# The MLP's down projection as seven quarter products, with the sums of weight quarters on POOL

## The chip, the cores and the metric

The kernel runs on one core of a Trainium2 chip. A run's time is device microseconds (us) from launch to end. The kernel before took 1097.14 us, the median of three runs (1096.91 to 1100.08). "Same" below means within 0.3% of it.

## What is computed

Two layers over 528 tokens (16 meta tokens and 512 of the sequence), width 1024, everything in float32. Each layer has an attention and pooling mixer, and then a gated MLP whose inner width is 2816 (22 blocks of 128). Cut to the part that is changed:

```python
xn = rms_norm(h, ffn_norm_g[l])
g = causal_dwconv(xn @ w_gate[l], conv_w[l], conv_b[l])          # width 3
h = h + (jax.nn.gelu(g, approximate=False) * (xn @ w_up[l])) @ w_down[l]
# after layer 1: return h[:, N_META:]
```

## The kernel before

The five engines run their own programs and meet through semaphores: PE multiplies, ACT and DVE do elementwise work, POOL does some more of it, SP only issues the loads. The order on each engine is the order in which the code is written; there is no scheduler.

**Every large product is three.** PE multiplies in fp32r, so each operand is kept as a rounded part and the rest: `w_hi` and `w_lo` for weights, `x_hi`/`x_lo` and `m_hi`/`m_lo` for activations. `dense` issues, for each block of 128 rows and 128 output features, hi·hi, hi·lo and lo·hi, each for both halves of the tokens (264 columns in a matmul), or in layer 1 in one matmul of 512 columns where only real tokens matter.

**Weight units.** Weights come in units of 256 output columns and up to 8 row blocks. SP loads unit u into `raw[u % 2]`; `split_hi` (ACT) writes `w_hi`, `split_lo` (DVE) subtracts and writes `w_lo`. A slot is rewritten when PE has finished the unit two before.

**The MLP.** Eleven turns i, each with four output tiles on PE: gate0, gate1, up0, up1 (PSUM slots 2, 3, 0, 1). DVE moves the gate tiles out of PSUM, ACT and DVE make the convolution in `conv`, ACT applies GELU, DVE moves the up tiles out, POOL multiplies (L774), and ACT and DVE split the product into `m_hi` and `m_lo`, which hold all 22 blocks. PE is meanwhile at the next turn.

**Down.** After the eleven turns, `w_down` is used in 12 units: four column pairs j, each with 8, 8 and 6 row blocks. The first units need only blocks 0 to 15 of `m`, so the chain behind the last up tile is under them. A finished tile is added to the residual `h` by DVE (`add_to_h`); in layer 0 ACT and DVE then at once make the next layer's operands `x_hi`, `x_lo` and the sum of squares (`gain_hi`, `gain_lo`, `square`, `add_square`), a column pair at a time.

Of the kernel before, what the change touches and what calls it, by code (L numbers as in the profile page):

```python
# [31 lines left out]
P = 128  # L32
# [18 lines left out]
U_DOWN = U_FFN + 2 * FI  # L51
DOWN_K = [(0, 8), (8, 16), (16, FT)]
UNITS = U_DOWN + len(DOWN_K) * (D_MODEL // UC)

# [11 lines left out]
class Psum:  # L66
# [7 lines left out]
    def __init__(self):  # L74
# [9 lines left out]
        order += [(f"down{t}", (2 + t) % 4) for t in range(KT)]  # L84
# [18 lines left out]
def build_trunk(nc, x, meta_tokens, attn_norm_g, w_in, q_norm_g, k_norm_g, sinks, w_pool, pool_scale,  # L103
# [5 lines left out]
    with ExitStack() as ctx:  # L109
# [64 lines left out]
        with ExitStack() as sc:  # L174
            m_hi = sb(sc, "m_hi", [P, FT, L], f32r)
            m_lo = sb(sc, "m_lo", [P, FT, L], f32r)
            gate = [sb(sc, f"gate{c}", [P, 2 + L]) for c in range(2)]
            conv = [sb(sc, f"conv{c}", [P, L]) for c in range(2)]
            up = [sb(sc, f"up{c}", [P, L]) for c in range(2)]
            cpar = sb(sc, "cpar", [P, 4, 2])  # L180
# [27 lines left out]
        down_used = sem("down_used")  # L208
# [32 lines left out]
        dve_par, dve_rot, dve_attn, dve_ffn = sem("dve_par"), sem("dve_rot"), sem("dve_attn"), sem("dve_ffn")  # L241
# [57 lines left out]
        def slot_turn(l, unit, pairs=0):  # L299

            return l * (UNITS // 2) + pairs + unit // 2

        def unit_rows(unit):
            if unit == U_POOL:
                return 2
            if unit >= U_DOWN:
                a, b = DOWN_K[(unit - U_DOWN) % 3]
                return b - a
            return 8

        def last_user_done(l, unit, i=0):


            old = unit - 2
            if old < 0:
                if old + UNITS == UNITS - 1:
                    name = f"down{KT - 1}"
                    return filled[ps.slot(name)], ps.before_last_layer(name, l) + 1
                return down_used, l * KT + 1
            if old >= U_DOWN:  # L320
                j, n = divmod(old - U_DOWN, 3)
                if n < 2:
# [8 lines left out]
            return filled[ps.slot(name)], ps.before(name, l, i) + 1  # L331


        def split_hi(act, l, unit, i=0, half=None):
# [11 lines left out]
        def split_lo(dve, l, unit, i=0, half=None):  # L346
# [3 lines left out]
            s, t, nk = unit % 2, slot_turn(l, unit, i), unit_rows(unit)  # L350
# [20 lines left out]
        def _(sp):  # L371
# [9 lines left out]
            def load(l, unit, src, i=0):  # L381

                s, n = unit % 2, unit_rows(unit)
                parts = [(raw[s][:, a:a + n // 2], src[:, a:a + n // 2]) for a in (n // 2, 0)]
                sp.wait_ge(lo_split[s], slot_turn(l, unit, i) + 1)
                for dst, part in parts:
                    sp.dma_start(dst, part).then_inc(raw_loaded[s], 16)

            for l in range(DEPTH):
# [10 lines left out]
                sp.wait_ge(lo_split[s], slot_turn(l, U_POOL) + 1)  # L400
# [5 lines left out]
                for j in range(D_MODEL // UC):  # L406
                    load(l, U_OUT + j, wo[:, :, j * UC:(j + 1) * UC])
                with sp.Fori(0, FI) as i:
                    load(l, U_FFN, wg[:, :, bass.ds(i * UC, UC)], i)
                    load(l, U_FFN + 1, wu[:, :, bass.ds(i * UC, UC)], i)  # L410
                for j in range(D_MODEL // UC):
                    for n, (a, b) in enumerate(DOWN_K):
                        load(l, U_DOWN + 3 * j + n, wd[:, a:b, j * UC:(j + 1) * UC])

# [10 lines left out]
        def _(pe):  # L425
# [40 lines left out]
            pe.sem_inc(down_used, 1)  # L466
# [25 lines left out]
            for l in range(DEPTH):  # L492
# [156 lines left out]
                with pe.Fori(0, 2) as i:  # L649
                    for t in range(4):  # L650
                        s, unit = open_slot(f"out{t}", l, i), U_OUT + t // 2
                        if t % 2 == 0:
                            pe.wait_ge(lo_split[unit % 2], slot_turn(l, unit, i) + 2)
                        dense(s, unit % 2, (t % 2) * P, rows, mix_hi, mix_lo, ready=mixed if t == 0 else None,
                              tail=l + 1 == DEPTH)\
                          .then_inc(filled[s], 1)


                def mlp_tiles(i, ready=None):
                    for n, name in enumerate(("gate0", "gate1", "up0", "up1")):  # L660
                        s, unit = open_slot(name, l, i), U_FFN + n // 2
                        if n % 2 == 0:
                            pe.wait_ge(lo_split[unit % 2], slot_turn(l, unit, i) + 2)
                        dense(s, unit % 2, (n % 2) * P, eight, x_hi, x_lo, ready=ready if n == 0 else None,
                              real=n >= 2 and l + 1 == DEPTH,
                              tail=n < 2 and l + 1 == DEPTH).then_inc(filled[s], 1)
                        if n == 0 and ready is not None:
# [711 lines left out]
```

## Time and profile before

| | |
|---|---|
| median of the runs | 1097.14 us |
| the profiled execution | 1099.67 us; its span, first to last instruction, is 1097.9 us |
| PE, DVE, ACT, POOL busy | 1061.1, 522.6, 471.5, 121.3 us |
| granted PE clock, mean | 0.987 of full speed |

A matmul is counted busy from its start to its modelled end, and matmuls overlap, so what one costs in a stream is the distance between two starts, not its duration. Each row of a timeline has the start (us from the span's start) and the duration; "x2" merges two instructions. In rows of a window the columns are named in the answer's second line: the stretch, its length, busy time and count, the granted clock, and the DMA share and rate.

### The profile page before, as it was taken

Reading aid. Unit: us, or ns where it says so; the run is one execution under the profiler, and the core shown is the slowest. Engines: PE = TensorE matmul, PEld = TensorE weight load, DVE = VectorE, ACT = ScalarE, POOL = GpSimd, SP = SyncE. Lnnn points to the kernel's source line nnn. Section 1 sums busy time; section 2 is a strip of 40 time slices with the busy share of each in tenths; the row PEclk is TensorE's granted clock in tenths of the full one; section 3 lists DMA queues with packets and bytes.
Section 4 is the critical chain, followed back from the end, with each engine's and each line's share of the span. In section 5 each row is a group of like instructions: output and inputs, shape, how many; then the busy total and the mean of one; then the engine's idle time right before and its main releaser. Section 6 shows DMA issues by size and latency. Waiting matters only on the chain.

```text
span 1097.9 us, 18457 instructions
## 1 busy us (share of the span) xinstructions
PE 1061.1 (97%) x7668; PEld 996.7 (91%) x7668; DVE 522.6 (48%) x690; ACT 471.5 (43%) x662; POOL 121.3 (11%) x121
## 2 busy tenths in 40 slices
PE   6898899999999999999999988999999999999997
PEld 6897799999999999999999878999988999888886
DVE  5566744545544545233336576455445454532221
ACT  5765536445434444122228655364354443421110
POOL 1252000011000011000002610000001100000000
PEclk8989999999999999999999999999999999999999
DMA  6311122232322232323231112322323232233212
GB/s 199 105 49 39 67 88 77 80 113 76 97 95 76 78 113 67 106 78 105 77 105 39 49 40 78 115 77 90 101 76 106 85 107 84 76 106 106 76 58 77
DMA packets 93518, 94.30 MB, mean 86 GB/s; under 512 B 3392, under 2 KB 91800, under 8 KB 93480
## 3 DMA queue, kind: packets, MB, share of 16 engines
q1 hardware_dynamic: 92768, 93.01, 26.6%
q0 software_dynamic: 400, 0.58, 0.2%
q8 instruction: 27, 0.44, 0.2%
q10 hardware_dynamic: 312, 0.18, 0.1%
q14 instruction: 11, 0.09, 0.0%
HBM read 91.65 MB, written 2.10 MB: 85 GB/s over the span
## 4 chain that ended last, share of the span: by engine, by line
PE 84%; ACT 7%; DVE 6%; DMA 1%; issue 1%; ACTq 0%; DVEq 0%
PE slot L451 82%; ACT probs L929 3%; DVE nmax L1180 1%; PE slot L507 1%; ACT w_hi L342 1%; DMA par_in<-in_conv_w 1%; DMA cst<-const_table 1%; DVE ms_work L1131 1%; DVE probs L1199 1%; DVE mix_lo L1215 0%; ACT x_hi L788 0%; DVE den L1191 0%; DVE sink_arg L1185 0%; ACT pool_hi L862 0%; ACT rot_s L854 0%
## 5 line engine op out<-in xcount | busy, mean ns | idle before, releaser
L451 PE MATMUL slot<-x_hi,w_hi 128*128 128x264 f32 (+2 forms) x1552 | 363.1, 301 | 6.8 <-DVE u_sb L1162 4.1
L451 PE MATMUL slot<-x_lo,w_hi 128*128 128x264 f32 (+2 forms) x1552 | 360.1, 299 | 0.0
L451 PE MATMUL slot<-x_hi,w_lo 128*128 128x264 f32 (+2 forms) x1552 | 359.3, 299 | 0.0
L353 DVE TENSOR_TENSOR w_lo<-raw,w_hi 128x2048 fp32r<-128x2048 f32 (+2 forms) x87 | 195.4, 2246 | 248.4 <-ACT w_hi L342 248.4
L342 ACT ACTIVATE w_hi<-raw 128x2048 fp32r<-128x2048 f32 (+3 forms) x89 | 160.8, 1807 | 263.1 <-PE slot L451 260.0
L451 PEld LDWEIGHTS slot<-x_hi,w_hi 128*128 128x128 f32 x1552 | 254.3, 191 | 19.2 <-DVE u_sb L1162 5.8
L451 PEld LDWEIGHTS slot<-x_lo,w_hi 128*128 128x128 f32 x1552 | 252.8, 191 | 7.3
L451 PEld LDWEIGHTS slot<-x_hi,w_lo 128*128 128x128 f32 x1552 | 252.4, 191 | 7.5
L451 PE MATMUL slot<-m_hi,w_lo 128*128 128x264 f32 (+1 forms) x528 | 140.7, 321 | 0.0
L451 PE MATMUL slot<-m_hi,w_hi 128*128 128x264 f32 (+1 forms) x528 | 140.4, 320 | 0.0
L451 PE MATMUL slot<-m_lo,w_hi 128*128 128x264 f32 (+1 forms) x528 | 140.3, 320 | 0.0
L774 POOL TENSOR_TENSOR up<-up,conv 128x528 f32<-128x528 f32 (+1 forms) x44 | 57.6, 1309 | 573.6 <-ACT conv L999 538.5
L994 ACT ACTIVATE conv<-gate,cpar 128x528 f32<-128x528 f32 (+1 forms) x44 | 36.2, 823 | 149.5 <-DVE gate L1088 75.6
L451 PEld LDWEIGHTS slot<-m_lo,w_hi 128*128 128x128 f32 x528 | 87.6, 188 | 7.9
L451 PEld LDWEIGHTS slot<-m_hi,w_lo 128*128 128x128 f32 x528 | 87.4, 188 | 7.6
L451 PEld LDWEIGHTS slot<-m_hi,w_hi 128*128 128x128 f32 x528 | 87.6, 188 | 7.4
L999 ACT ACTIVATE conv<-conv 128x528 f32<-128x528 f32 (+1 forms) x44 | 28.1, 639 | 73.7 <-DVE conv L1297 73.7
L451 PE MATMUL slot<-mix_hi,w_hi 128*128 128x264 f32 (+1 forms) x256 | 52.0, 284 | 0.0
L451 PE MATMUL slot<-mix_hi,w_lo 128*128 128x264 f32 (+1 forms) x256 | 51.9, 284 | 0.0
L451 PE MATMUL slot<-mix_lo,w_hi 128*128 128x264 f32 (+1 forms) x256 | 51.7, 284 | 0.0
L1088 DVE TENSOR_TENSOR gate<-slot,rinv 128x528 f32<-128x528 f32 x22 | 15.6, 708 | 56.6 <-PE slot L451 56.5
L1287 DVE TENSOR_TENSOR gate<-slot,rinv 128x516 f32<-128x516 f32 x22 | 15.3, 696 | 55.3 <-PE slot L451 55.2
(144 smaller groups left out, 941.7 us busy)
## 6 DMA issues: line engine op xcount, KB each, us to landing
raw<-in_w_gate SPq DMA_DIRECT2D x44, 512.0 KB, 4.6
raw<-in_w_up SPq DMA_DIRECT2D x44, 512.0 KB, 4.5
raw<-in_w_down SPq DMA_DIRECT2D x32, 512.0 KB, 4.4
raw<-in_w_in SPq DMA_DIRECT2D x19, 512.0 KB, 5.0
raw<-in_w_out SPq DMA_DIRECT2D x16, 512.0 KB, 4.1
raw<-in_w_down SPq DMA_DIRECT2D x16, 384.0 KB, 3.6
x_in<-in_x SPq DMA_DIRECT2D x4, 512.0 KB, 7.0
out<-y_out SPq DMA_DIRECT2D x8, 256.0 KB, 3.0
```

Of the source, the lines that this page charges most:

```text
L342: ins = nc.scalar.activation(w_hi[s][:, a:b], raw[s][:, a:b], ACT.Copy)
L353: ins = nc.vector.tensor_tensor(w_lo[s][:, a:b], raw[s][:, a:b], w_hi[s][:, a:b].bitcast(f32), ALU.subtract)
L451: ins = nc.tensor.matmul(out_part, w[ws][:, r, cols], a[:, k, tokens], start=first and n == 0 and w is w_hi and a is a_hi, stop=end and w ...
L507: ins = nc.tensor.matmul(slot[s][:, 0, 2 * b:2 * b + 2], head_sq[:, b, :], cst[:, C_BLK:C_BLK + P:HEAD_DIM], start=True, stop=True)
L774: nc.gpsimd.tensor_tensor(up[c][:, t0:], up[c][:, t0:], conv[c][:, t0:], ALU.mult)\
L929: ins = nc.scalar.activation(probs[:, y, t, 0:nk], slot[s][:, t // 2, col], ACT.Exp, bias=nm[:, y, t:t + 1], scale=q_scale[:, b, t // 2, t ...
L994: nc.scalar.activation(conv[c][:, t0:], gate[c][:, 2 + t0:], ACT.Identity, bias=cpar[:, 3, c:c + 1], scale=cpar[:, 2, c:c + 1]).then_inc(t ...
L999: nc.scalar.activation(conv[c][:, t0:], conv[c][:, t0:], ACT.Gelu).then_inc(gelu_ready, 1)
L1088: nc.vector.tensor_tensor(tok(dst), halves(s), tok(rinv[:]), ALU.mult).then_inc(evac[s], 1)
L1131: rot.link(nc.vector.reciprocal(ms_work[:], ms_work[:]))
L1180: ch.link(nc.vector.tensor_reduce(nmax[:, y].rearrange("p (a t) -> p a t", a=2), view, op=ALU.max, axis=AX.X, negate=True))
L1287: nc.vector.tensor_tensor(tok(gate[c][:, 2 + TAIL0:]), tail_halves(s), tok(rinv[:, TAIL0:]), ALU.mult).then_inc(evac[s], 1)
```

## The change

Down is done in three chunks of the inner width instead of at the end: after turns 0 to 3, 4 to 7 and 8 to 10 (`CHUNKS`), and in each chunk for four column pairs (`down` units, which the text calls d0 to d3). A unit of n turns is a 2 by 2 product of quarters: two blocks of output features, two halves of the tokens, and the two row blocks of each turn. It is computed with seven products of quarters (`PRODUCTS`, P1 to P7) where `dense` made eight; four of the seven weight operands and four of the seven activation operands are sums of quarters.

- POOL makes the weight sums (`operand_sums`: four instructions a unit, into one buffer `w_sum`), ACT and DVE split the seven weight operands in four groups (`operand_hi`, `operand_lo`, n = 0 to 3).
- DVE makes the activation sums of every turn (`middle_sums`, four instructions), ACT and DVE split into `m_op` in three parts.
- In the last turn of each chunk DVE, not POOL, does the gated product (`gated`).
- P1 and P6 and P7 share one PSUM bank and accumulate in it, P5 and P3 another. DVE adds each product to `h` (`add_product`), and the next product into that bank waits for this.
- All loops are written out; the tap of `conv` is a scaled Copy (before: Identity with bias), and the bias goes into GELU. `m_sum` lies in the buffer of `conv`.
- In layer 1 a quarter is 256 tokens wide, in layer 0 264.

```diff
-DOWN_K = [(0, 8), (8, 16), (16, FT)]
+CHUNKS = [(0, 4), (4, 8), (8, FI)]
+for c, (a, b) in enumerate(CHUNKS):
+    PLAN += [(kind, i) for i in range(a, b) for kind in ("gate", "up")] + [("down", 4 * c + j) for j in range(4)]
++PRODUCTS = {"P1": (0, 0, (0, 0), ((0, 0),)), "P2": (0, 1, (0, 1), ((0, 0),)), "P3": (2, 2, (1, 0), ((0, 1),)),
+            "P4": (3, 6, (1, 1), ((1, 0),)), "P5": (1, 3, (1, 0), ((1, 1),)), "P6": (1, 4, (0, 0), ((0, 1),)),
+            "P7": (2, 5, (0, 0), ((1, 0), (1, 1)))}
+ORDER = ("P1", "P5", "P2", "P6", "P3", "P4", "P7")
+FIRST_ORDER = ("P1", "P2", "P5", "P4", "P6", "P3", "P7")
```

In `PRODUCTS` each entry has the group of weight operands, the activation operand, the PSUM bank and the quarters of `h` it is added to. On PE:

```diff
+                def product(name, unit, kks, first, last):
...
+                    pe.wait_ge(opnd_lo[op], d + 1)
+                    if first and name in ("P6", "P3", "P7"):
+                        pe.wait_ge(h_added, added_count(d, {"P6": "P1", "P3": "P5", "P7": "P6"}[name]))
+                    for kk in kks:
+                        for n, (w, a) in enumerate(((0, 0), (0, 1), (1, 0))):
+                            ins = nc.tensor.matmul(dst, part[s][w][:, wn, kk], m_op[a][:, m, kk, 0:width],
+                                                   start=first and kk == kks[0] and n == 0 and name in ("P1", "P2", "P4", "P5"),
+                                                   stop=last and kk == kks[-1] and n == 2, skip_group_check=True)
...
+                        for name in FIRST_ORDER[0:4]:
+                            product(name, unit, range(n - 1), True, False)
+                        for name, parts in (("P1", 1), ("P2", 2), ("P5", 3), ("P4", 3)):
+                            pe.wait_ge(mlo_ready, 3 * (l * FI + i1 - 1) + parts)
+                            product(name, unit, range(n - 1, n), False, True)
+                        for name in FIRST_ORDER[4:]:
+                            product(name, unit, range(n), True, True)
```

On POOL, for every down unit (`operand_sums`):

```diff
+                    if part == 0:
+                        pool.wait_ge(raw_loaded[s], load_turn(l, unit) * 32 + 32)
+                        if d > 0:
+                            pool.wait_ge(opnd_lo[1], d)
+                        nc.gpsimd.tensor_tensor(sums[:, 0], a21, a22, ALU.add).then_inc(sum_ready, 1)
+                        pool.wait_ge(sum_ready, 4 * d + 1)
+                        nc.gpsimd.tensor_tensor(sums[:, 1], sums[:, 0], a11, ALU.subtract).then_inc(sum_ready, 1)
+                        return
+                    if d > 0:
+                        pool.wait_ge(opnd_lo[2], d)
+                    pool.wait_ge(sum_ready, 4 * d + 2)
+                    nc.gpsimd.tensor_tensor(sums[:, 2], a12, sums[:, 1], ALU.subtract).then_inc(sum_ready, 1)
+                    nc.gpsimd.tensor_tensor(sums[:, 3], a21, a11, ALU.subtract).then_inc(sum_ready, 1)
```

Three places in the engines' orders follow. First, **DVE in layer 0, from the second tap to the end of a turn of the loop.** Before (every turn; `up0` and `up1` are the up tiles, L353 is `split_lo`):

```order
L1294 SCALAR_TENSOR_TENSOR conv1<-gate1,cpar,conv1 128x528 [waits tap2_ready]
L1297 SCALAR_TENSOR_TENSOR conv1<-gate1,cpar,conv1 128x528 [waits dve_ffn]
L1088 TENSOR_TENSOR up0<-slot0,rinv 128x528 [waits filled0]
L1088 TENSOR_TENSOR up1<-slot1,rinv 128x528 [waits filled1]
L353 TENSOR_TENSOR w_lo1<-raw1,w_hi1 128x2048 [waits hi_split1]
L1312 TENSOR_TENSOR m_lo<-up0,m_hi 128x528
L1312 TENSOR_TENSOR m_lo<-up1,m_hi 128x528
```

After, in the last turn of chunk 0 (L445 is `operand_lo`, L1515 `gated`, `work` holds `up` and `conv`; `w_ext` and `w_lo` hold the operands):

```order
L445 TENSOR_TENSOR w_lo0<-w_sum,w_hi0 128x1024 [waits opnd_hi1]
L1293 TENSOR_TENSOR work<-slot0,rinv 128x528 [waits filled0,mlo_ready]
L1515 TENSOR_TENSOR work<-work 128x528 [waits evac0,gelu_ready]
L445 TENSOR_TENSOR w_lo0<-w_sum,w_hi0 128x1024 [waits opnd_hi2]
L445 TENSOR_TENSOR w_ext_lo0<-raw0,w_ext_hi0 128x512 [waits opnd_hi3]
L445 TENSOR_TENSOR w_ext_lo1<-raw1,w_ext_hi1 128x1024 [waits opnd_hi0]
L445 TENSOR_TENSOR w_ext_lo1<-raw1,w_ext_hi1 128x512 [waits opnd_hi3]
L1293 TENSOR_TENSOR work<-slot1,rinv 128x528 [waits filled1,mlo_ready]
L1515 TENSOR_TENSOR work<-work 128x528 [waits evac1,gelu_ready]
L1525 TENSOR_TENSOR work<-work 128x264 [waits m_last]
```

Four `operand_lo` now stand between the first and the second up tile, and the activation sums (from L1525) and three splits follow before PE may finish d0.

Second, **POOL in that last turn.** Before, a turn's two L774 (`up<-up,conv`) are all its work. After:

```order
L928 TENSOR_TENSOR work<-work 128x528 [waits evac1,gelu_ready]
L908 TENSOR_TENSOR w_sum<-raw0 128x512 [waits raw_loaded0]
L910 TENSOR_TENSOR w_sum<-w_sum,raw0 128x512 [waits sum_ready]
L915 TENSOR_TENSOR w_sum<-raw0,w_sum 128x512 [waits sum_ready]
L916 TENSOR_TENSOR w_sum<-raw0 128x512
L908 TENSOR_TENSOR w_sum<-raw1 128x512 [waits opnd_lo1,raw_loaded1]
L910 TENSOR_TENSOR w_sum<-w_sum,raw1 128x512 [waits sum_ready]
L915 TENSOR_TENSOR w_sum<-raw1,w_sum 128x512 [waits sum_ready,opnd_lo2]
L916 TENSOR_TENSOR w_sum<-raw1 128x512
```

The sums of d1 (raw1) start once DVE has made d0's group 1, and their second pair once it has made group 2: among the four `operand_lo` shown above.

Third, **DVE in the last chunk of layer 0, from d2 to d3.** Before, at the same stage (L1262 adds a finished tile to `h`, L1043 is `gain_lo`, L1053 `add_square`):

```order
L1262 TENSOR_TENSOR h<-slot2,h 128x528 [waits filled2]
L1262 TENSOR_TENSOR h<-slot3,h 128x528 [waits filled3]
L1043 SCALAR_TENSOR_TENSOR x_lo<-h,par_all,x_hi 128x528 [waits xhi_ready] x2
L1053 TENSOR_TENSOR sumsq<-sq 128x528 [waits sq_ready]
L353 TENSOR_TENSOR w_lo0<-raw0,w_hi0 128x2048 [waits hi_split0]
```

After (L1553 adds a product to `h`, L1248 is `gain_lo`, L1261 `add_square`; slots 2 and 3 belong to d2, 0 and 1 to d3):

```order
L445 TENSOR_TENSOR w_ext_lo1<-raw1,w_ext_hi1 128x384 [waits opnd_hi3]
L1553 TENSOR_TENSOR h<-slot3,h 128x264 [waits h_added,prod_done]
L1553 TENSOR_TENSOR h<-slot2,h 128x264 [waits h_added,prod_done]
L1553 TENSOR_TENSOR h<-slot2,h 128x264
L1248 SCALAR_TENSOR_TENSOR x_lo<-h,par_all,x_hi 128x528 [waits xhi_ready]
L1261 TENSOR_TENSOR sumsq<-sumsq,sq 128x528 [waits sq_added,sq_ready]
L1248 SCALAR_TENSOR_TENSOR x_lo<-h,par_all,x_hi 128x528 [waits xhi_ready]
L1261 TENSOR_TENSOR sumsq<-sumsq,sq 128x528 [waits sq_added,sq_ready]
L1553 TENSOR_TENSOR h<-slot0,h 128x264 [waits h_added,prod_done]
```

The next layer's splits stand between the last addition of d2 and the addition of d3's P1, for which PE's P6 of d3 waits.

## Rows read from the trace of the kernel before

**Rows 1.** The page's part 1, busy time of three engines.
```profile
PE 1061.1 (97%) x7668; PEld 996.7 (91%) x7668; DVE 522.6 (48%) x690; ACT 471.5 (43%) x662; POOL 121.3 (11%) x121
```
**Rows 2.** The chain that ended last, its two longest pieces: start, us, what.
```profile
182.72 392.46 PE slot L451 x3216
...
721.94 365.62 PE slot L451 x2064
```
**Rows 3.** Windows of PE: down in both layers, two gate tiles.
```profile
435.10:563.20 128.10, 128.10 (x1058) 1.00 0.28 92
965.50:1087.40 121.90, 121.90 (x529) 1.00 0.22 71
...
761.29:772.88 11.59, 11.59 (x97) 1.00 0.28 90
```
**Rows 4.** Groups by form: what one costs on ACT, DVE and POOL (mean ns).
```profile
L342 ACT ACTIVATE w_hi<-raw 128x2048 fp32r<-128x2048 f32 x75 | 143.3, 1911 | 195.3 <-PE slot L451 192.2 <-DMA cst<-const_table 3.0
...
L1043 DVE SCALAR_TENSOR_TENSOR x_lo<-h,par_all,x_hi 128x528 fp32r<-128x528 f32 x32 | 23.6, 761 | 0.1
...
L1294 DVE SCALAR_TENSOR_TENSOR conv<-gate,cpar,conv 128x528 f32<-128x528 f32 x22 | 16.8, 762 | 0.0
...
L1312 DVE TENSOR_TENSOR m_lo<-up,m_hi 128x528 f32 x22 | 14.5, 695 | 0.0
...
L1003 ACT ACTIVATE m_hi<-up 128x528 f32 x22 | 12.7, 626 | 0.0
...
L1056 DVE TENSOR_TENSOR sumsq<-sumsq,sq 128x528 f32<-128x528 f32 x24 | 16.9, 704 | 1.2 <-ACT sq L795 0.7
...
L1162 DVE TENSOR_TENSOR u_sb<-slot,rinv 128x264 f32<-128x264 f32 x12 | 5.1, 426 | 0.0
```
**Rows 5.** The source lines of two POOL operations: ns min/median/max.
```profile
L757 POOL TENSOR_TENSOR run_b<-run_a x4: 1067/1067/1070, 76.7 to 628.0; 128x528 f32<-128x528 f32 x4
...
L774 POOL TENSOR_TENSOR up<-up,conv x44: 1287/1306/1339, 198.0 to 966.4; 128x528 f32<-128x528 f32 x22, 128x512 f32<-128x512 f32 x22
```
**Rows 6.** Timeline of DVE in the last turn of layer 0, and PE's next start.
```profile
423.58 0.71 DVE L1088 TENSOR_TENSOR gate<-slot,rinv 128x528 f32<-128x528 f32 x1 [5.17 <-PE slot L451]
427.00 2.29 DVE L353 TENSOR_TENSOR w_lo<-raw,w_hi 128x2048 fp32r<-128x2048 f32 x1 [2.70 <-ACT w_hi L342]
...
435.33 0.71 DVE L1088 TENSOR_TENSOR up<-slot,rinv 128x528 f32<-128x528 f32 x1 [2.46 <-PE slot L451]
...
435.13 0.40 PE L451 MATMUL slot<-m_hi,w_hi 128*128 128x264 f32 x2
```
**Rows 7.** Timeline of DVE and POOL together, in layer 1's projections.
```profile
599.25 0.71 DVE L1107 TENSOR_TENSOR v_T<-head,sq 128x528 f32<-128x528 f32 x1
599.30 1.83 POOL L739 TENSOR_TENSOR rot_c<-head,sq 128x528 f32<-128x528 f32 x1 [4.50 <-DVE k_dup L1141]
...
599.88 3.41 DVE L353 TENSOR_TENSOR w_lo<-raw,w_hi 128x2048 fp32r<-128x2048 f32 x1
```
```profile
609.91 2.36 DVE L353 TENSOR_TENSOR w_lo<-raw,w_hi 128x2048 fp32r<-128x2048 f32 x1 [0.94 <-ACT w_hi L342]
...
610.20 3.27 POOL L739 TENSOR_TENSOR rot_c<-head,sq 128x528 f32<-128x528 f32 x1
```
**Rows 8.** Windows of all engines around a fall of the clock.
```profile
595.95:599.30 3.35, 2.43 (x22) 2.24 (x21) 2.86 (x5) 2.89 (x4) 0.00 (x1) 1.00 0.00 0
599.30:602.75 3.45, 3.45 (x17) 3.45 (x17) 3.45 (x2) 2.70 (x5) 1.83 (x2) 0.51 0.02 5
```
**Rows 9.** Timeline of PE before and after that fall.
```profile
597.21 2.14 PE L507 MATMUL slot<-cst,head_sq 128*128 128x2 f32 x18 [0.92 <-ACT head_sq L838]
...
601.88 0.64 PE L451 MATMUL slot<-x_hi,w_hi 128*128 128x264 f32 x2
602.32 0.61 PE L451 MATMUL slot<-x_lo,w_hi 128*128 128x264 f32 x2
```
**Rows 10.** DMA issues by line: KB each, us from issue to landing.
```profile
raw<-in_w_down SPq DMA_DIRECT2D x32, 512.0 KB, 4.4
```

More of the change, by code:

```diff
@@ L647, in mixed @@
                         pe.wait_ge(evac[ps.slot(name)], ps.before(name, l) + 1)
[L649 to L656, printed above, removed]
@@ L674, in _ @@
[L674 to L689 removed]
+                width = half_tokens(l)[0]
@@ L768, in _, with operand_sums @@
                 t0 = N_META if l + 1 == DEPTH else 0
-                with pool.Fori(0, FI) as i:
+                def operand_sums(unit, part):
+                    d, s = down_turn(l, unit), unit % 2
+                    r = unit_rows(unit) // 2
+                    rows = raw[s][:, 0:2 * r].rearrange("p (k h) (c m) -> p h c k m", h=2, c=2)
+                    a11, a12, a21, a22 = rows[:, 0, 0], rows[:, 1, 0], rows[:, 0, 1], rows[:, 1, 1]
+                    sums = w_sum[:, :, 0:r]
+                    if part == 0:
[11 more added lines that the diff above has]
+                    nc.gpsimd.tensor_tensor(sums[:, 3], a21, a11, ALU.subtract).then_inc(sum_ready, 1)
+                for i in range(FI):
+                    if is_last(i):
+                        for j in range(4):
+                            for part in range(2):
+                                operand_sums(UNIT_OF["down", 4 * chunk_of(i) + j], part)
+                        continue
                     for c in range(2):
@@ L1005, in _ @@
[L1005 to L1013 removed]
+                width, (na, nb) = half_tokens(l)
@@ L1315, in _ @@
[L1315 to L1326 removed]
+                width, (na, nb) = half_tokens(l)
@@ new lines, in add_product @@
+                def add_product(unit, name):
+                    d, s, j = down_turn(l, unit), unit % 2, PLAN[unit][1] % 4
+                    pair, half = PRODUCTS[name][2]
+                    bank = slot[(2 if s == 0 else 0) + pair][:, half, 0:width]
+                    targets = PRODUCTS[name][3]
+                    dve.wait_ge(prod_done, product_count(d, name))
+                    dve.wait_ge(h_added, added_count(d, name) - len(targets))
+                    for c, part in targets:
+                        rows = h[:, 2 * j + c, (na, nb)[part]]
+                        nc.vector.tensor_tensor(rows, bank, rows, ALU.add).then_inc(h_added, 1)
@@ L1328, in _ @@
+                conv_link.close()
             for t in range(SEQ // P):
```

480 lines of the change are left out of this document (333 added, 147 removed).

## The prediction

> **What bounds the kernel now.** I read the page's busy times first: PE 97% of the span, DVE 48%, ACT 43%, POOL 11% [rows 1]. Busy PE alone proves little, so the chain that ended last came next: two of its pieces, 392.46 and 365.62 us, are nothing but matmuls of L451 in a row, and both run through the MLP and down [rows 2]. No other engine is waited for there, so in these stages a matmul less is time less, and a wait added on PE is time more, with nothing to hide it. The windows give the price of a matmul in a stream [rows 3]: layer 0's down issues 1056 matmuls of 264 columns in 128.1 us, 0.1213 us each; layer 1's issues 528 of 512 columns in 121.9 us, 0.2308 each; two gate tiles of layer 1 are 96 matmuls of 258 columns in 11.59 us up to the next tile's start, 0.1207 each. Half the columns cost more than half the time: this matters, since layer 1 now gets quarters of 256 columns.
>
> **What PE is relieved of.** Per layer: 4 column pairs x 7 products x 11 turns x 3 = 924 matmuls. Layer 0: 1056 - 924 = 132 fewer, x 0.1213 = 16.0 us. Layer 1: 528 x 0.2308 = 121.9 against 924 of 256 columns. No row has 256. The slope between 264 and 512 columns is 0.00044 us a column: from the 258 columns' 0.1207 it makes 0.1198, from the 264 columns' 0.1213 it makes 0.1178. I take the nearer size, 0.1198, so 110.7 and a gain of 11.2 us; 0.1178 would give 13.0, and 0.1207 without a slope 10.4. Together **27.2 us saved**.
>
> On this the Trainium skill has a rule (TensorE: Matmul & The Clock Gate, section Back-to-back issue gap): at full clock a matmul takes its columns over 2.4 GHz plus about 2.5 ns. An estimate by that page is 0.109 us for 256 columns, 9.9 us more gain than in my sum. The trace disagrees at the nearest size: 264 columns take 0.1213 us here where the rule makes 0.1125.
>
> **What PE newly waits for: the end of a chunk.** Before, the last up tile's chain lies under the first units of down. Now d0 may do only 3 x 3 matmuls of each of P1, P2, P5, P4 (36; in the 3-turn chunk 24) before it needs the last turn. Call T0 the moment PE starts d0, and X the moment, after T0, at which DVE starts on the second up tile. Costs of one [rows 4, 6]: DVE 2.29 us for 2048 elements and 0.695 for 528, so 1.22, 0.95, 0.68, 0.42 and 1.25 for 1024, 768, 512, 264 and 1056; ACT 1.911 and 0.626, so 1.07 for 1056. Behind X: up tile 0.7, gated 0.7, four sums of 264 in a chain 1.85, two splits 1.1, then the last split of 1056 elements (ACT's part lies beside) 1.25 and handovers, 5.75 in all. PE has 36 + 6 matmuls for that time, 5.1 us; with 24 + 6, 3.65. So **a stall is X + 0.65 (4 turns) or X + 2.1 (3 turns)**.
>
> X: from the second gate tile's landing to T0 there are 435.13 - 423.58 = 11.55 us [rows 6]. In it DVE now does that tile 0.7, four taps 3.05, two operand_lo 2.44, the first up tile and gated 1.4, and four operand_lo 1.22 + 0.68 + 1.22 + 0.68 = 3.8: 11.4 us. So DVE alone would be just in time, X = 0.2. But POOL's sums of d1 fall exactly among them. In [rows 7] DVE and POOL, both reading two operands of SBUF, take turns whole instructions long: POOL's rot_c is issued at 599.30 and gets in when v_T ends; w_lo, issued at 599.88, lasts 3.41 instead of 2.29; and at 610.20 it is POOL that lasts 3.27 behind a w_lo. The Trainium skill states this (SBUF — State Buffer, section Who interferes with whom): a DVE instruction with two SBUF inputs and a GpSimd one that reads SBUF exclude each other for a whole instruction. The trace agrees, by the 1.1 us of that w_lo. Without that rule the boundary stalls would be the lower bound below, 18 us less.
>
> A sum has 512 elements: 1.04 us by the shifted sum of one tensor, 1.29 by the product of two [rows 5]; I take two of each, 4.65 us for four, all of it in DVE's way except 0.65 under the first up tile: X = 0 + 3.8 or so, 1.45 in the 3-turn chunk (smaller sums, and DVE has 1.4 us spare). In layer 1 the gap is 0.5 us shorter (up tiles of 24 x 0.2308), X 4.2 and 1.7. Stalls: layer 0 2 x 4.4 + 3.6 = 12.4, layer 1 2 x 4.8 + 3.7 = 13.3: **25.7 us**. Bounds: X without any blocking, 3.4 + 3.8 = 7.2; with every sum at 1.29, 28.
>
> **Inside the units.** A unit of 4 turns is 84 matmuls, 10.2 us on PE; DVE has eight additions out of PSUM of 0.43 [rows 4] and operands of 4.0, 7.4 us, and up to three blocks of 1.0 to 1.3. P6 needs the addition of P1, due 4.4 us into the unit; stepping through d1 to d3 it comes 0 to 1.3 us late once per chunk: 0.5 each for four chunks, 2. With 3 turns PE needs 7.65, DVE 6.8 plus blocks: late once by 1.4 in layer 1. **3.4 us.** ACT (3584 elements a unit, 3.7 us) and the loads (two of 512 KB in parallel, 4.4 us to land [rows 10], room of a unit) are covered.
>
> **Layer 0's last chunk.** There DVE does two gain_lo and two squares, 2 x (0.76 + 0.70) = 2.9 us [rows 4], between d1 and d2 and again between d2 and d3, in front of the addition of P1 that P6 waits for. From the end of d0: DVE is through d1's additions and d2's operands at 11.75, through the norm work at 14.0 (the first has one square less), adds P1 at 14.45; P6 was due at 10.9: 3.6 us. Again for d3: 2.1. Then d3's own norm work ends 1.0 us late for the next layer's k tile. **6.7 us**; without blocking 4.
>
> **The clock.** PE ran at 0.51 of full clock (1.2 GHz) for 3.45 us after a stretch of 3.35 us that was thin, a 0.92 us pause and 18 tiny matmuls [rows 8, 9]. A boundary's stall is thin for some 5 us. At low clock a matmul costs 0.22 us [rows 9], so 3.45 us hold 15.7 instead of 28.4, a loss of 1.5 us. I count two such falls, **3.1 us**; none to six, 0 to 9.
>
> **Costed at nothing:** the written-out loops, since the loops cost PE nothing (3216 matmuls through eleven turns took 392.46 us, 0.122 each [rows 2]); the table loads and cpar copies that go (ACT and DVE idle there); sums and splits in middle turns, which PE's next 17 us of tiles hide: were that cover gone, 3.1 us a turn. The last additions: +0.2.
>
> **Sum.** Profiled execution 1099.67 - 27.2 + 25.7 + 3.4 + 6.7 + 3.1 + 0.2 = 1111.6; it was 2.5 us over the median of the runs, so **1109 us**.
>
> **The cases.** A difference under 0.3% (3.3 us) can't be told from none.
> 1. As summed, 1098 to 1120, likeliest 1109: 0.6. For it: [rows 7]; against: the alternation is read from few instructions.
> 2. POOL's sums slip past DVE, being done before the four operand_lo or in DVE's PSUM work: then 1099.67 - 27.2 + 7.2 + 1 + 4 + 0.2 = 1084.9, less 2.5: 1082. The side is decided at the stalls: below 27 us in all the change gains. For it: 3.2 us of the four sums of d1 would have to fit under up tile and taps; against: the sums of d1 may not start before operand_lo 1 of d0. 0.22, and it reaches up to 1094.
> 3. Savings and stalls cancel, 1094 to 1100: 0.08 beyond the edges of the others.
> 4. Low clock at all boundaries and a DVE that falls behind in every unit (at 3 turns it has 6.8 + 1.6 of 7.65 us): 9 - 3.1 + 6 more, 1121: 0.1.
>
> The range leaves out the outer halves of cases 2 and 4: 1083 to 1121; case 1's own is 1098 to 1120. Faster 0.24, same 0.08, slower 0.68.
>
> **What would show it.** PE with 6 gaps of 3 to 5 us just after the up tiles of turns 3, 7 and 10 of each layer, released by DVE's m_op_lo; operand_lo instructions of 1024 elements of 2.2 us beside 1.2; P6 of d2 and d3 in layer 0 waiting for an addition to h; matmuls of 256 columns at 0.1195. Wrong would be: operand_lo never above 1.3, an up1 taken out of PSUM within 0.5 us of its landing, or waits of PE under 27 us in sum.

## The result, and the profile after

The changed kernel takes **1122.07 us** (median of 4 runs, 1120.37 to 1123.01); the kernel before, in the same comparison, 1097.61 (4 runs, 1096.91 to 1100.08). The ratio is 1.0217, with a 95% interval of 1.0196 to 1.0238: slower by 2.2%. The profiled execution took 1123.01 us, its span is 1121.0 us, the mean granted clock 0.972.

The page's part 1 of the changed kernel, which answers to [rows 1], and its row of the granted clock:

```profile
PE 1055.4 (94%) x7932; PEld 1008.6 (90%) x7932; DVE 743.3 (66%) x1038; ACT 473.3 (42%) x714; POOL 263.5 (24%) x205
...
PEclk9989999999999998999899999999989999899989
```

In the first row each engine has its busy time, the share of the span and its instructions; the second gives the granted clock in tenths of full speed over 40 slices of the span. DVE is busy for 221 us more and POOL for 142. PE is busy for 6 us less, although it should have lost 27 us of work. Its waits, by what ended them (us in all, times, longest):

```profile
PE slot L787 <- DVE m_op_lo L1539: 24.1, 12, 4.5
...
PE slot L787 <- DVE h L1553: 6.2, 5, 3.0
```

L787 is the matmul of a down product. None of these waits existed before. `m_op_lo` is the last part of the activation operands of a turn; a wait for `h` is one for an addition of a product. Windows of PE over the six chunks of down, each from the first down matmul to the next turn's tile, with the answer's sum:

```profile
269.64:317.91 48.27, 44.01 (x338) 0.93 0.28 90
...
531.03:572.12 41.09, 34.63 (x255) 0.92 0.27 88
...
sum 273.71, PE 242.52; mean PE 40.42
```

Down took 128.1 + 121.9 = 250.0 us before [rows 3] and takes 273.7 now. The rest of the span, 1097.9 - 250.0 and 1121.0 - 273.7, is 847.9 and 847.3 us: **all of the change lies in down**. (The last of the six windows also holds a wait of 0.9 us ahead of the output's tiles, which [rows 3] leaves out; it shifts this by 1 us.) Now windows of PE inside down: a stretch in the first wait and behind it, the next one, and then the corresponding stretch of the five other chunks (fourth figure: granted clock).

```profile
277.60:284.40 6.80, 5.93 (x25) 0.50 0.00 0
284.40:291.00 6.60, 6.60 (x56) 1.00 0.01 1
```
```profile
421.00:427.80 6.80, 6.38 (x27) 6.07 (x28) 3.33 (x6) 2.87 (x4) 0.00 (x0) 0.50 0.01 2
537.00:543.80 6.80, 6.00 (x28) 5.81 (x27) 3.13 (x7) 1.85 (x3) 0.00 (x0) 0.50 0.00 0
827.20:834.00 6.80, 6.39 (x29) 6.08 (x29) 3.26 (x6) 2.97 (x4) 0.00 (x0) 0.50 0.01 2
963.70:970.50 6.80, 4.28 (x18) 3.99 (x19) 5.38 (x11) 4.53 (x5) 0.00 (x0) 0.50 0.00 0
1079.70:1086.60 6.90, 6.22 (x30) 5.92 (x29) 3.35 (x7) 1.98 (x3) 0.00 (x0) 0.51 0.00 0
```

Behind the wait of every chunk PE runs at half clock, 1.2 GHz, for 6.8 us, and in the first of these stretches it issues 25 matmuls where the next 6.6 us hold 56. The first waits of the six are 3.88, 3.89, 1.80, 4.52, 4.52 and 2.42 us long, the shorter ones in the chunks of three turns, and behind six matmuls each has a second one of 0.37 to 0.80 us. Timeline of PE around the first of them (start, duration, what, idle time before and its releaser):

```profile
273.93 0.28 PE L787 MATMUL slot<-m_op_hi,w_ext_lo 128*128 128x264 f32 x1
278.09 0.59 PE L787 MATMUL slot<-m_op_hi,w_ext_hi 128*128 128x264 f32 x1 [3.88 <-DVE m_op_lo L1539]
...
280.16 0.59 PE L787 MATMUL slot<-m_op_hi,w_hi 128*128 128x264 f32 x1 [0.38 <-DVE m_op_lo L1539]
...
284.48 0.28 PE L787 MATMUL slot<-m_op_lo,w_hi 128*128 128x264 f32 x1
```

A matmul costs 0.22 us in that stretch and 0.12 behind it. And the two engines that make the wait, DVE and then POOL, in the last turn of the first chunk (PE starts d0 at 269.64):

```profile
265.59 0.70 DVE L1293 TENSOR_TENSOR work<-slot,rinv 128x528 f32<-128x528 f32 x1
...
266.40 1.28 DVE L1515 TENSOR_TENSOR work<-work 128x528 f32<-128x528 f32 x1
267.61 2.30 DVE L445 TENSOR_TENSOR w_lo<-w_sum,w_hi 128x1024 fp32r<-128x1024 f32 x1
269.83 4.61 DVE L445 TENSOR_TENSOR w_ext_lo<-raw,w_ext_hi 128x512 fp32r<-128x512 f32 x3
274.37 0.69 DVE L1293 TENSOR_TENSOR work<-slot,rinv 128x528 f32<-128x528 f32 x1
...
278.84 1.26 DVE L1539 TENSOR_TENSOR m_op_lo<-work,m_op_hi 128x1056 fp32r<-128x1056 f32 x1 [0.19 <-ACT m_op_hi L1183]
```
```profile
265.82 1.30 POOL L908 TENSOR_TENSOR w_sum<-raw 128x512 f32<-128x512 f32 x1 [9.60 <-DVE w_lo L445]
267.19 1.63 POOL L910 TENSOR_TENSOR w_sum<-w_sum,raw 128x512 f32<-128x512 f32 x1
269.99 1.68 POOL L915 TENSOR_TENSOR w_sum<-raw,w_sum 128x512 f32<-128x512 f32 x1 [1.16 <-DVE w_lo L445]
271.62 2.28 POOL L916 TENSOR_TENSOR w_sum<-raw 128x512 f32<-128x512 f32 x1
```

The gated product takes 1.28 us instead of 0.71, the operand of 1024 elements 2.30 instead of 1.22, the three behind it 4.61 instead of some 2.4. DVE comes to the second up tile (274.37) 4.73 us after PE started d0, and no row between shows it idle: it is held up, not waiting for its inputs. The whole run shows it in groups by form, the operands longer and the additions from PSUM not; a mean holds alone-running and delayed instructions together:

```profile
L445 DVE TENSOR_TENSOR w_lo<-w_sum,w_hi 128x1024 fp32r<-128x1024 f32 x32 | 50.3, 1571 | 8.1 <-ACT w_hi L438 8.1
L1553 DVE TENSOR_TENSOR h<-slot,h 128x264 f32<-128x264 f32 x96 | 40.1, 428 | 24.0 <-PE slot L787 21.8
```

### The profile page after: what moved, and what is told of

Same layout as the page of the kernel before. It is cut to its first block, busy times and chain, and to the rows that moved or that the text cites. A ratio compares the mean times of both kernels' runs of the same rounds, so it can differ in the third digit from the quotient of the medians.

```text
span 1121.0 us, 19011 instructions
## 1 busy us (share of the span) xinstructions
PE 1055.4 (94%) x7932; PEld 1008.6 (90%) x7932; DVE 743.3 (66%) x1038; ACT 473.3 (42%) x714; POOL 263.5 (24%) x205
## 4 chain that ended last, share of the span: by engine, by line
PE 61%; DVE 21%; ACT 10%; issue 5%; POOL 2%; DMA 1%; SPq 0%; DVEq 0%; ACTq 0%; POOLq 0%
PE slot L552 45%; PE slot L787 13%; ACT probs L1090 3%; DVE w_ext_lo L445 2%; DVE w_lo L445 2%; ACT w_hi L400 2%; DVE h L1553 1%; DVE m_op_lo L1539 1%; ACT m_op_hi L1183 1%; DVE work L1515 1%; DVE work L1525 1%; DVE work L1527 1%; DVE work L1529 1%; DVE work L1530 1%; DVE nmax L1385 1%
## 5 line engine op out<-in xcount | busy, mean ns | idle before, releaser
L411 DVE TENSOR_TENSOR w_lo<-raw,w_hi 128x2048 fp32r<-128x2048 f32 (+1 forms) x63 | 146.3, 2322 | 86.0 <-ACT w_hi L400 86.0
L400 ACT ACTIVATE w_hi<-raw 128x2048 fp32r<-128x2048 f32 (+2 forms) x65 | 118.3, 1820 | 142.0 <-PE slot L552 89.5
L787 PE MATMUL slot<-m_op_hi,w_hi 128*128 128x264 f32 (+1 forms) x352 | 106.0, 301 | 9.2 <-DVE h L1553 6.2
L1553 DVE TENSOR_TENSOR h<-slot,h 128x264 f32<-128x264 f32 (+1 forms) x192 | 79.4, 424 | 49.3 <-PE slot L787 45.0
L787 PE MATMUL slot<-m_op_lo,w_hi 128*128 128x264 f32 (+1 forms) x352 | 104.5, 297 | 0.0
L787 PE MATMUL slot<-m_op_hi,w_lo 128*128 128x264 f32 (+1 forms) x352 | 104.3, 296 | 0.0
L787 PE MATMUL slot<-m_op_hi,w_ext_hi 128*128 128x264 f32 (+1 forms) x264 | 77.4, 293 | 21.0 <-DVE m_op_lo L1539 21.0
L787 PEld LDWEIGHTS slot<-m_op_hi,w_hi 128*128 128x128 f32 x352 | 71.9, 204 | 11.8 <-issue 7.0
L445 DVE TENSOR_TENSOR w_lo<-w_sum,w_hi 128x1024 fp32r<-128x1024 f32 (+1 forms) x48 | 69.1, 1439 | 11.1 <-ACT w_hi L438 11.1
L787 PE MATMUL slot<-m_op_hi,w_ext_lo 128*128 128x264 f32 (+1 forms) x264 | 76.3, 289 | 0.0
L787 PE MATMUL slot<-m_op_lo,w_ext_hi 128*128 128x264 f32 (+1 forms) x264 | 76.1, 288 | 0.0
L787 PEld LDWEIGHTS slot<-m_op_hi,w_ext_hi 128*128 128x128 f32 x264 | 51.2, 194 | 23.2 <-DVE m_op_lo L1539 23.1
```

The costliest lines, as they stand in the source:

```text
L400: ins = nc.scalar.activation(w_hi[s][:, a:b], raw[s][:, a:b], ACT.Copy)
L411: ins = nc.vector.tensor_tensor(w_lo[s][:, a:b], raw[s][:, a:b], w_hi[s][:, a:b].bitcast(f32), ALU.subtract)
L445: nc.vector.tensor_tensor(dst, src, hi.bitcast(f32), ALU.subtract).then_inc(opnd_lo[n], 1)
L787: ins = nc.tensor.matmul(dst, part[s][w][:, wn, kk], m_op[a][:, m, kk, 0:width], start=first and kk == kks[0] and n == 0 and name in ("P1" ...
L1553: nc.vector.tensor_tensor(rows, bank, rows, ALU.add).then_inc(h_added, 1)
```

## The account of down

At full clock 924 matmuls of 264 columns cost 924 x 0.1213 = 112.1 us. For 256 columns the trace now has a price: 88 matmuls in a row start between 855.73 and 866.00 us, 0.118 each, so 924 cost 109.0. Together 221.1 us, 28.9 less than before. The low clock: the six windows above hold 157 matmuls at 0.22 instead of 0.12, 15.7 us; 14.5 when each distance between two starts is counted by itself, without what a restart behind a wait adds at either clock; I use this below. What is left, 273.7 - 221.1 - 14.5 = 38.1 us, is waiting and starting again after a wait. The page lists 24.1 + 6.2 us of waits for down and the 0.9 ahead of the output; the other 6.9 were not taken apart.

| down, us | forecast | measured |
|---|---|---|
| work saved | 27.2 | 28.9 |
| waits and restarts (forecast: boundaries 25.7, units 3.4, norm 6.7, end 0.2) | 36.0 | 38.1 |
| low clock | 3.1 | 14.5 |
| sum | +11.9 | +23.7 |

## The experiments

All are edits of the changed kernel; their times are to be read against 1122.07 us. Ratios are to the kernel before, run on the same chip. There it took 1096.78 us beside experiments 1 to 4, 1098.33 beside 5 to 8 and 1099.32 beside 9, against 1097.61 beside the changed kernel, so a difference of 1 to 3 us between two medians is not clear by itself.

**1. No sums of weight quarters.** The operands are rounded and split from plain quarters, and neither POOL nor anyone makes `w_sum`. It leaves out the four weight sums of each unit; its matmuls and splits are as many and as large.

```diff
-                        for j in range(4):
-                            for part in range(2):
-                                operand_sums(UNIT_OF["down", 4 * chunk_of(i) + j], part)
...
-                act.wait_ge(sum_ready, 4 * d + 2 * n)
```

> The changed kernel without the sums of weight quarters: POOL makes none, and the two operand groups that were sums are split from plain quarters, so the down projection is not the reference's; every split, matmul and addition keeps its size and place. Theory A (POOL's sums and DVE's splits exclude each other, and that makes the stall at a chunk's end): DVE reaches the second up tile within 0.5 us of its landing, the operand_lo of 1024 elements are all 1.22 us, PE's waits for m_op_lo fall from 24 us to 6 to 9, those for additions to h from 6 to about 2. If the clock then stays up, 1122 - 17 - 4 - 14 = 1087; if it still falls at every boundary, about 1100. Rival B (the work that DVE has itself between the gate and the up tile makes the stall, POOL only lies beside it): waits for m_op_lo stay above 20 us and the time above 1117.

Measured: **1082.49 us** (ratio 0.9875, 0.9858 to 0.9892), 4.5 us under the 1087 that was expected if the clock stays up. Its waits of PE, the timeline of DVE in the same last turn (PE starts d0 at 267.58), and the sum of its six windows of down:

```profile
PE slot L786 <- DVE m_op_lo L1535: 6.6, 8, 0.9
```
```profile
261.98 0.71 DVE L1289 TENSOR_TENSOR work<-slot,rinv 128x528 f32<-128x528 f32 x1
...
263.42 1.22 DVE L444 TENSOR_TENSOR w_lo<-raw,w_hi 128x1024 fp32r<-128x1024 f32 x1
264.56 2.42 DVE L444 TENSOR_TENSOR w_ext_lo<-raw,w_ext_hi 128x512 fp32r<-128x512 f32 x3
267.85 0.71 DVE L1289 TENSOR_TENSOR work<-slot,rinv 128x528 f32<-128x528 f32 x1 [0.88 <-PE slot L551]
```
```profile
sum 234.78, PE 226.31; mean PE 37.72
```

DVE now waits for the up tile instead of being late for it. Down costs 38.9 us less than in the changed kernel: the four sums and what they delay, low clock included, are the whole loss and more. The clock does not stay up everywhere: in layer 0's chunk of three turns, behind two waits of 0.92 and 0.81 us, a stretch at half clock is left.

```profile
521.70:525.10 3.40, 3.36 (x15) 0.50 0.00 0
```

The median lands on case 2's 1082. This kernel has no sums of weight quarters at all, where case 2 had them slip past DVE, so it bears out that case's sum (its profiled execution less closely: 1080.51 against 1084.9) and not its premise.

**2. The sums on DVE.** The same four instructions, issued by DVE behind the gate tiles and between the additions to `h`.

```diff
-                        nc.gpsimd.tensor_tensor(sums[:, 0], a21, a22, ALU.add).then_inc(sum_ready, 1)
+                        nc.vector.tensor_tensor(sums[:, 0], a21, a22, ALU.add).then_inc(sum_ready, 1)
...
                         for c in range(2):
                             gate_tile(i, c)
+                            if is_last(i):
+                                operand_sums(down[0], c)
```

> The changed kernel with the four sums of a unit on DVE instead of POOL, put where DVE has room (d0's between the two gate tiles, d1's after the addition of P6, d2's and d3's after the splits that free the buffer). Theory A: no blocks, X back to about 0.2, waits for m_op_lo 6 to 9 us; but DVE then has 10.1 of 10.2 us of work in a unit and 2.7 us more in front of some additions, so waits for h rise to 8 to 15. 1095 to 1108 in all. Rival B (DVE's total is what counts): 1122 or more. This is also the question of the change's last words: POOL in place of DVE gains if this is slower than 1122, and loses if it is faster.

Measured: **1108.70 us** (1.0109, 1.0092 to 1.0126), 0.7 us above the 1095 to 1108 that were expected. The waits moved:

```profile
PE slot L787 <- DVE h L1570: 14.7, 9, 2.5
PE slot L787 <- DVE m_op_lo L1556: 7.0, 10, 0.9
```

DVE has the work, and PE waits in the units for additions that come late. At the boundaries the long wait is gone, though the operands are still sums that must be made first: it was POOL's work beside DVE that made it, not the waiting for the sums. The low clock there is gone too: the windows of three chunks show a clock of 1.00, and those of the other three 0.96, where the changed kernel has 0.91 to 0.93. The three falls that are left stand behind waits for additions. In this order POOL in place of DVE costs 13.4 us.

**3. The wait filled.** PE issues 33 (in the short chunk 16) matmuls of 264 columns into a free bank where it would wait for the last turn's operands; nobody reads them.

```diff
+                        pe.wait_ge(evac[ps.slot("up0")], ps.before("up0", l, i1 - 1) + 1)
+                        for _ in range(33 if n == 4 else 16):
+                            nc.tensor.matmul(slot[0][:, 0, 0:HALF], x_hi[:, 0, 0:P], x_hi[:, 0, 0:HALF],
+                                             start=True, stop=True)
```

> The changed kernel, and while PE would wait for the last turn's operands in d0 it does 33 (three-turn chunk: 16) matmuls of 264 columns into a PSUM bank that nobody reads: the waits stay, only PE isn't idle in them. Theory C (the idle 4 to 5 us at the six boundaries is what brings the clock to half for 6.8 us each, and that costs some 14 us): granted clock 1.00 in all of the MLP, L787 matmuls always at 0.12 us, and 1122 - 14 + 1 = 1107 to 1110. Rival D (the half clock has another cause, or the filling matmuls run at half clock themselves): 1120 or more.

Measured: **1109.97 us** (1.0135, 1.011 to 1.016). PE does 164 matmuls more and the kernel is 12.1 us faster. Window of PE at the place of the first fall:

```profile
277.60:284.40 6.80, 5.97 (x46) 1.00 0.00 1
```

46 matmuls where there were 25. All six windows of down have a clock of 1.00, and their sum is 260.07 us, 13.6 less than in the changed kernel. The wait is still there, only filled, and DVE and POOL do the same as before; so 12 us of the loss (13.6 in the profiled executions) are the clock's alone. This is the run that shows the failed step.

**4. One late operand instead of four.** Only d0's group 3 stays between the two up tiles; d0's group 2 and d1's groups 0 and 3 move behind, among the additions of d0.

```diff
-                            for unit, n in ((down[0], 2), (down[0], 3), (down[1], 0), (down[1], 3)):
-                                operand_lo(dve, l, unit, n)
+                            operand_lo(dve, l, down[0], 3)
                             up_tile(i, 1)
...
                     for name in FIRST_ORDER[0:2]:
                         add_product(down[0], name)
+                    operand_lo(dve, l, down[0], 2)
```

> The changed kernel with another order on DVE alone: of the four operand_lo between the first and the second up tile only d0's group 3 stays; d0's group 2 and d1's groups 0 and 3 come after the last turn's splits, among the additions of d0, where PE needs them later. POOL's sums stay, and those of d1's second pair wait for d0's group 2, so they leave the critical stretch too. Theory A: X about 0.2 to 1, waits for m_op_lo 6 to 12 us; the clock may stay up at the four-turn boundaries; 1087 to 1100. Rival E (the blocks only move, to the splits and additions of d0): waits for h or operands rise by what is gained, 1115 to 1122.

Measured: **1101.87 us** (1.0048, 1.0031 to 1.0064): 20 us gained, 1.9 us above the 1087 to 1100 of the theory. The waits:

```profile
PE slot L787 <- DVE h L1553: 13.1, 9, 3.1
PE slot L787 <- DVE m_op_lo L1539: 6.6, 8, 0.9
```

The boundaries' own waits are down to those of experiment 1, and none of them loses clock; one stretch of 3.4 us at half clock is left, behind a wait of 3.15 us for an addition. 7 us of the gain were given back at the next place in DVE's order: what was moved stands in front of additions for which P6 waits.

**5. Layer 0's norm work later.** `gain_lo` and the squares of each column pair move behind the addition of the next unit's P6 or P5, for which PE would wait.

```diff
-                        if final and l + 1 < DEPTH:
-                            next_low(j - 1)
...
                         add_product(unit, "P6")
+                        if final and l + 1 < DEPTH and j == 2:
+                            next_low(0)
```

> The changed kernel with one part moved on DVE, in layer 0's last chunk alone: the next layer's norm work of a column pair comes after the addition of P6 of the next unit (d2), or after the additions of P1 and P5 (d3), no longer in front of the addition of P1. Theory: the two waits of P6 for an addition there (3.29 and 1.13 us in the changed kernel's trace) go, 0.5 to 1.5 us come back at d3 or at the next layer's first tile: 1122 - 3 = 1119. Rival: DVE is simply overloaded in this chunk, and the wait turns up at another product: 1121 to 1123.

Measured: **1118.74 us** (1.0198, 1.018 to 1.0215): 3.3 us less, the expected time, with an interval that overlaps the changed kernel's 1.0196 to 1.0238. In the changed kernel's timeline of PE they are

```profile
558.86 0.36 PE L787 MATMUL slot<-m_op_hi,w_hi 128*128 128x264 f32 x1 [3.01 <-DVE h L1553]
567.64 0.36 PE L787 MATMUL slot<-m_op_hi,w_hi 128*128 128x264 f32 x1 [0.85 <-DVE h L1553]
```

3.9 us where 3.6 and 2.1 were forecast, the second much shorter. How much of the 3.3 us is theirs is not shown: in the profiled execution the edited chunk takes 40.34 us instead of 41.09, 0.7 less, and the last chunk of layer 1, which the edit does not touch, is 0.8 us shorter (37.80), with a fall of the clock of 3.4 us instead of 6.8.

**6. A second order for DVE.** As 4, with d1's groups 2 and 3 later still, inside d1's own additions, and with the addition of d1's P6 ahead of d2's group 1.

```diff
                         add_product(unit, "P1")
+                        if j == 1:
+                            operand_lo(dve, l, unit, 2)
                         add_product(unit, "P5")
+                        if j == 1:
+                            operand_lo(dve, l, unit, 3)
```

> The reordered kernel of before (only d0's group 3 between the up tiles), with d1's groups 2 and 3 moved behind the first additions of d1, and the addition of P6 of d1 ahead of d2's group 1, since that kernel's P6 of d1 waited 1.7 to 2.2 us at every boundary. Theory: these waits go, 5 to 9 us of its 1101.9 in all: 1093 to 1097. Rival: DVE with its blocks has more work than a unit has time, and the wait moves to P7 or to d2: 1100 or more.

Measured: **1103.32 us** (1.0034, 1.0015 to 1.0052). A miss: the waits only moved again (12.6 us for `h`, 12 times), and four chunks now hold a stretch at half clock, three behind waits of 2.27 to 3.69 us for an addition and one behind the two short waits of a boundary (0.93 and 0.79). The wait ahead of the first of them:

```profile
434.87 0.56 PE L787 MATMUL slot<-m_op_hi,w_hi 128*128 128x264 f32 x1 [2.27 <-DVE h L1553]
```

**7. Experiments 5 and 6 together.**

> Both: the second order and the moved norm work. If the two terms are independent, the second order's time less 3 us: 1090 to 1094. If they are one overload of DVE, no more than 1 us less than the second order alone.

Measured: **1097.79 us** (0.9992, 0.9977 to 1.0008), the kernel before's time, and above the 1090 to 1094 that independent terms would have given. It is 5.5 us less than experiment 6, and 10.1 less by the windows of down (246.58 against 256.69), but not by the norm work alone. The second chunk of layer 0, in which both kernels have the same orders, in experiment 6 and here:

```profile
405.95:452.44 46.49, 43.23 (x338) 0.96 0.30 92
```
```profile
406.05:449.12 43.07, 41.95 (x338) 1.00 0.32 100
```

The wait of 2.27 us of experiment 6 and the fall behind it are missing here, and likewise in layer 1's first chunk (46.15 and 42.74 us). So 6.8 of the 10.1 us lie where nothing was changed, 2.8 in the edited chunk (41.28 and 38.51).

**8. The short chunk first.** Experiment 7 with chunks of 3, 4 and 4 turns, so that the norm work falls into a chunk with longer units.

```diff
-CHUNKS = [(0, 4), (4, 8), (8, FI)]
+CHUNKS = [(0, 3), (3, 7), (7, FI)]
```

> As the last, with chunks of 3, 4 and 4 turns instead of 4, 4 and 3, so that the chunk in which DVE also has the norm work has units of 10.2 us instead of 7.65. Theory: 1 to 3 us less than the last, 1088 to 1092, and faster than the kernel before (1097). Rival: the longer first stretch of the later chunk costs as much as it saves: the same within 1 us.

Measured: **1093.41 us** (0.996, 0.9945 to 0.9974): faster than the kernel before by 0.4%, and 2.6% under the changed kernel. The gain on experiment 7 is 4.4 us where 1 to 3 were expected, and the time 1.4 above the expected 1088 to 1092. Waits of PE and the sum of its windows of down:

```profile
PE slot L787 <- DVE m_op_lo L1539: 6.6, 8, 0.9
...
PE slot L787 <- DVE h L1553: 3.2, 8, 0.7
```
```profile
sum 243.49, PE 231.73; mean PE 38.62
```

Of the 28.9 us saved 6.5 are kept; 22.4 are still waits, restarts and one stretch of 3.4 us at half clock. The way there from 1122.07, as differences of medians: DVE's order (experiment 6) 18.8 us, experiment 7 a further 5.5, the chunks 4.4; the share of the norm work in the 5.5 is not shown.

**9. Experiment 8 with the sums on DVE.**

```diff
                         operand_lo(dve, l, nxt, 0)
+                        operand_sums(nxt, 0)
                         add_product(unit, "P2")
+                        operand_sums(nxt, 1)
```

> The kernel e8_reorder2_norm_chunks (1093.4 us), with the four sums of each down unit made by DVE: those of the first unit behind the two gate tiles of the last turn, those of the others between the additions of the unit before. Theory P (POOL's sums delay DVE by more than they spare it, wherever they fall): a sum of 512 elements takes DVE about 0.7 us, 2.7 us a unit, and POOL's sum beside it makes DVE's instructions 1 us longer; in the order of the change the move to DVE was worth 13 us. What is left of waits in down is 20 us, about 10 of them at the chunks' ends; if the half of that is POOL's, the kernel takes 1085 to 1091. Rival Q (once the late operands no longer stand at the chunks' ends, POOL blocks only work with room): DVE's additions come later by 2.7 us a unit that were spare before, no gain, 1093 to 1099.

Measured: **1106.53 us** (1.0069, 1.0055 to 1.0083). Neither theory: 13.1 us slower than experiment 8, when the move to DVE, with other places for the sums, gained 13.4 in experiment 2. Its waits, DVE's timeline in the first chunk with the operand for which PE waits until 259.19, and its group of 1024 elements:

```profile
PE slot L787 <- DVE w_ext_lo L445: 10.4, 6, 1.8
```
```profile
255.91 0.55 DVE L1539 TENSOR_TENSOR w_sum<-raw 128x384 f32<-128x384 f32 x1
256.49 0.56 DVE L1541 TENSOR_TENSOR w_sum<-w_sum,raw 128x384 f32<-128x384 f32 x1
257.15 0.56 DVE L1546 TENSOR_TENSOR w_sum<-raw,w_sum 128x384 f32<-128x384 f32 x1
257.63 0.55 DVE L1547 TENSOR_TENSOR w_sum<-raw 128x384 f32<-128x384 f32 x1
258.10 0.95 DVE L445 TENSOR_TENSOR w_ext_lo<-raw,w_ext_hi 128x768 fp32r<-128x768 f32 x1
```
```profile
L445 DVE TENSOR_TENSOR w_lo<-w_sum,w_hi 128x1024 fp32r<-128x1024 f32 x32 | 38.6, 1217 | 0.0
```

Without POOL no operand is delayed (1217 ns against the changed kernel's 1571), and yet PE waits more: 2.2 us of sums (2.7 in the long chunks) stand in front of the operand that PE needs next. Only one placement of DVE's sums was tried in each order, so this tells that POOL is the better place in this order as it is written, not that DVE could not be placed better.

## Why the prediction was wrong, by its own steps

The direction was right, the size was not: 11.9 us slower was forecast, 24.5 was measured (23.3 between the two profiled executions), 1.1 us beyond the range.

- **Work saved: right.** 28.9 against 27.2; the 256 columns cost 0.118, the lower of the two slopes. On this the rule of the Trainium skill (TensorE: Matmul & The Clock Gate, section Back-to-back issue gap) gives an estimate of 0.109; the page has that rule for an isolated matmul, and the trace disagrees again. For a stream of weight loads and matmuls the same section has about 131 ns at 512 columns; the trace of the kernel before has 0.2308 us [rows 3].
- **Boundary stalls: right in mechanism, near in size.** d1's four sums delayed DVE by 0.6 (gated product), 1.1 (first operand) and 2.2 us (the next three), 3.8 as forecast. X was 4.7 because DVE was late by 0.9 besides: it came to the first up tile 4.05 us ahead of PE's start of d0, in experiment 1 5.6 us. The end of d0's chain then took what was forecast, and PE stood for 3.88 us ahead of the first held-back matmul and 0.38 ahead of a later product, 4.3 in all against 4.4. That these agree is luck in part: the forecast's stall was a delay of the 43rd matmul, and this one starts at 280.16 where 42 at full clock would have ended at 274.74, 5.4 us later, which is the forecast's own X + 0.65 with X at 4.73. The missing 1.1 us are restarts and six matmuls at half clock between the two waits. Taken so, the six boundaries come to 30.1 us against 25.7; the waits listed for `m_op_lo` to 24.1. Experiment 1 takes the cause away and the long wait with it. The Trainium skill (SBUF — State Buffer, section Who interferes with whom) says that DVE with two SBUF inputs and GpSimd exclude each other for whole instructions; the trace agrees by 2.30 against 1.22 us, and by `h<-slot,h`, which has one input in PSUM and stays at 0.428 us.
- **Units and norm work: right in kind, too high in size.** Waits for `h` sum to 6.2 us where 3.4 + 6.7 were forecast; the second norm wait was 0.85 instead of 2.1. That all waits and restarts together come to 38.1 us, near the forecast's 36.0, is luck in part: restarts were not in the forecast and make up for it.
- **The clock: this step failed.** "I count two such falls, 3.1 us; none to six, 0 to 9." There are six falls, one for each boundary, and each lasts 6.8 us, not the 3.45 that one fall of [rows 8] had; together 14.5 us, beyond even the upper bound. With 14.5 in its place the prediction's own sum gives 1123.0 against a profiled execution of 1123.01; the errors of the other terms, 1.7 us more saved and 2.1 us more waited, nearly cancel. Two mistakes are in it. The stalls were forecast as alike at all six places and yet only two were given a fall. And the price was read off one row as if every fall had its length, although the trace of the kernel before holds a longer one, in its first 100 us:

```profile
56.60:63.40 6.80, 6.80 (x33) 0.50 0.09 26
```

Experiment 3 shows the term by itself, 12.1 us. One reason why it is less than 14.5: some of the slow matmuls stand between the two waits of a boundary, where speed only lengthens the second wait (0.38 us in the changed kernel's first chunk, 0.82 in experiment 3's). Where the long waits of the boundaries go, most of their falls go, too: experiment 4 has none at a boundary, experiments 1 and 8 have one of 3.4 us each, both in a chunk of three turns.
- **The cases.** Case 4 put low clock everywhere at 0.1, and named the time nearest to the result, 1121. That was luck in part: its six falls were priced at 9 us, and the 6 us for a DVE that falls behind in every unit did not come. Case 2 (0.22) was wrong in its premise.

What stays open: a second `w_sum` buffer, which would let POOL make the sums of d1 early, under the turns, was not tried. Why one wait brings a fall and another of its length does not, and why a fall lasts 3.4 or 6.8 us, no run shows. Where 22 us of experiment 8 go in small pieces (listed waits for down are 10.2 of them) was not taken apart.

## What to carry to other kernels

A wait of 2 to 4.5 us on a PE that was never waiting can cost more than its length: price a half-clock stretch behind every one of them at the longest that the trace shows, not the shortest, and call that a bound. Not every such wait has one: the 3.01 us wait for an addition in the changed kernel had none. When work moves to POOL, look up which DVE instructions with two operands in SBUF stand beside it at a point where PE waits; the price is not POOL's time but the wait for a POOL instruction in each of them, some 1.1 us here. And whether POOL or DVE is the better place depends on the order around it: here moving the sums to DVE gained 13 us in one order and lost 13 in another.

## What the runs showed that I had not expected

- Filling a wait with work that nobody needs made the kernel 12.1 us faster (experiment 3).
- The half-clock stretch behind the waits of a boundary (first waits of 1.8 to 4.5 us) lasted 6.8 us at all six places of the changed kernel, twice the 3.45 of [rows 8]; in experiment 5 the last of these places had the same first wait, 2.42 us, and 3.4 us of low clock. Behind the 2.3 us wait of experiment 6 it lasted 3.4.
- The length of one wait does not tell. In experiment 2 waits of 1.8 us for an addition, at the same place of four chunks, were followed by a fall in layer 1 and by none in layer 0. The two short waits of a boundary (0.9 and 0.8 us) were followed by 3.4 us of low clock in one chunk each of experiments 1, 6, 7, 8 and 9, and by none in experiment 4.
- The first matmul after a wait holds the next one back: 278.09 to 278.47, 0.38 us, where the others at that clock are 0.22 apart.
- The middle sums of ordinary turns are blocked as well, by the sums of d0, which POOL starts at 248.56: in the changed kernel's timeline of DVE

```profile
250.68 1.52 DVE L1525 TENSOR_TENSOR work<-work 128x264 f32<-128x264 f32 x1
252.23 1.40 DVE L1527 TENSOR_TENSOR work<-work 128x264 f32<-128x264 f32 x1
```

instead of 0.43. PE's next tiles hide it: outside down nothing is lost.
